# The last adaLN gate of a decoder block: its partial rows summed into a column layout instead of a broadcast row

## What is computed

```python
mod = jax.nn.silu(c) @ w_ada[l] + b_ada[l]
sh_m, sc_m, gt_m, sh_f, sc_f, gt_f = [m[:, None, :] for m in jnp.split(mod, 6, axis=-1)]
...
x = x + gt_m * rms_norm(mix, g_post_mix[l])
h = rms_norm(x, g_pre_ffn[l]) * (1.0 + sc_f) + sh_f
ff = peer_ffn(h, peer_wq[l], peer_k1[l], peer_k2[l], peer_u[l], peer_v[l])
x = x + gt_f * rms_norm(ff, g_post_ffn[l])
```

## Time and profile before

| what | value |
|---|---|
| median of three runs | 1837.81 us (1836.92 to 1838.18) |
| the profiled execution, its own time | 1838.79 us |
| span from its first to its last instruction | 1836.8 us |
| TensorE busy with matmuls | 1788.0 us, 97% of the span |
| VectorE busy | 1586.4 us, 86% |
| ScalarE busy | 825.0 us, 45% |
| GpSimd busy | 207.1 us, 11% |
| DMA | 617.98 MB, mean 336 GB/s |
| mean granted TensorE clock | 0.994 of full speed |

### The profile page before, as it was taken

How to read it: one execution, slowest core, us unless ns; L and a number is a source line. 1 busy time by engine, 2 the same in 40 slices (tenths; PEclk the granted TensorE clock), 3 DMA queues, 4 the chain that set the end, 5 groups by cost and what they waited for, 6 DMA issues and landing times.

```text
span 1836.8 us, 28930 instructions
## 1 busy us (share of the span) xinstructions
PE 1788.0 (97%) x9874; PEld 1565.2 (85%) x9874; DVE 1586.4 (86%) x2605; ACT 825.0 (45%) x1187; POOL 207.1 (11%) x193
## 2 busy tenths in 40 slices
PE   6999999998999999999999999989999999999998
PEld 6878888444999999999999999988888888888886
DVE  4669899966678999999999999987888888888887
ACT  3011222302635555333566666554555455555544
POOL 1000000110000000111121111121111111111110
PEclk9999999999999999999999999999999999999999
DMA  9998766798686677998999999999999999999995
GB/s 385 421 422 340 273 252 251 290 421 365 229 324 252 230 250 252 365 338 325 339 352 363 359 362 363 347 364 342 382 368 371 364 375 366 363 368 376 363 373 211
DMA packets 96785, 617.98 MB, mean 336 GB/s; under 512 B 11697, under 2 KB 20433, under 8 KB 25041
## 3 DMA queue, kind: packets, MB, share of 16 engines
q1 hardware_dynamic: 60048, 415.26, 59.0%
q0 software_dynamic: 25408, 184.58, 26.3%
q10 hardware_dynamic: 11266, 17.32, 2.5%
HBM read 600.26 MB, written 16.79 MB: 336 GB/s over the span
## 4 chain that ended last, share of the span: by engine, by line
PE 71%; DVE 13%; DMA 11%; issue 4%; ACT 1%; DVEq 0%; SPq 0%; ACTq 0%
PE ps L1310 32%; PE ps L960 12%; PE ps L967 8%; DMA raw<-in_w_ada 7%; PE ps L1005 6%; PE ps L1168 4%; PE ps L1114 3%; DVE big L1390 2%; PE ps L1016 2%; PE ps L1262 2%; DVE raw L1415 2%; DVE w_low L1368 2%; DMA big<-in_u_rows,row_ix 2%; DMA big<-in_w_gate_f 1%; DVE big L1471 1%
## 5 line engine op out<-in xcount | busy, mean ns | idle before, releaser
L673 ACT ACTIVATE w_hi<-raw 128x1024 fp32r<-128x1024 f32 x520 | 551.4, 1061 | 499.9 <-PE ps L1310 245.3
L1368 DVE TENSOR_TENSOR w_low<-raw,w_hi 128x1024 fp32r<-128x1024 f32 x520 | 631.8, 1220 | 96.5 <-ACT w_hi L673 89.6
L1310 PE MATMUL ps<-w_hi,a 128*128 128x512 f32 x1536 | 391.3, 390 | 5.6 <-DVE a L1823 5.6
L960 PE MATMUL ps<-a,w_hi 128*128 128x384 f32 x1856 | 374.1, 342 | 0.9 <-issue 0.8
L1310 PEld LDWEIGHTS ps<-w_hi,a 128*128 128x128 f32 x1536 | 289.1, 188 | 66.2 <-issue 5.8
L960 PEld LDWEIGHTS ps<-a,w_hi 128*128 128x128 f32 x1856 | 315.9, 189 | 1.9 <-issue 1.7
L1310 PE MATMUL ps<-w_low,a 128*128 128x512 f32 x1024 | 274.8, 390 | 0.0
L967 PEld LDWEIGHTS ps<-a,w_low 128*128 128x128 f32 x1856 | 237.7, 191 | 10.1 <-DVE w_low L1368 9.5
L967 PE MATMUL ps<-a,w_low 128*128 128x192 f32 x1856 | 241.8, 272 | 4.0 <-DVE w_low L1368 3.6
L1310 PEld LDWEIGHTS ps<-w_low,a 128*128 128x128 f32 x1024 | 192.6, 188 | 40.7 <-DVE w_low L1368 0.7
L1415 DVE CUSTOM_DVE_ANT_0 raw<-raw,big 128x2048 f32<-128x2048 f32 x64 | 146.2, 2290 | 66.7 <-DMA raw<-in_w_ada 64.0
(11 more groups left out here) (224 smaller groups left out, 1665.4 us busy)
## 6 DMA issues: line engine op xcount, KB each, us to landing
raw<-in_peer_u SPq DMA_DIRECT2D x128, 1024.0 KB
raw<-in_peer_v SPq DMA_DIRECT2D x128, 1024.0 KB
early<-in_w_front SPq DMA_DIRECT2D x56, 1024.0 KB, 9.0
raw<-in_w_ada POOLq DMA_DIRECT2D x48, 1024.0 KB, 9.1
raw<-in_w_ada SPq DMA_DIRECT2D x32, 1024.0 KB, 12.6
raw<-in_peer_wq SPq DMA_DIRECT2D x16, 1024.0 KB
big<-in_w_gate_f SPq DMA_DIRECT2D x16, 1024.0 KB, 7.2
gel_saved<-stage ACTq DMA_DIRECT2D x64, 192.0 KB
```

Source lines behind the costliest of these rows:

```text
L673: act.activation(w_hi[:, h % 2, :], raw[:, s % RING, :], ACT.Copy).then_inc(hi_ready, 1)
L960: done = pe.matmul(ps[:, b % 2, 0:2 * TD].rearrange("p (m t) -> p m t", m=2), w_hi[:, ph.nth(j) % 2, k * P:(k + 1) * P], a_pair[:, kc, :, ...
L1310: done = pe.matmul(ps[:, 4 * tt + 2 * (j % 2) + n, :], a, w[:, n * 512:(n + 1) * 512], start=i is None and blk == 0 and m in (0, 2), stop= ...
L1368: dve.tensor_tensor(w_low[:, s % RING, :], raw[:, s % RING, :], w_hi[:, h % 2, :].bitcast(F32), ALU.subtract).then_inc(lo_ready, 1)
```

## The change

The partial rows are summed the other way round: the partial rows are the stationary operand and a single column of ones is the moving one. Sixteen products take the place of four. Product kc loads the 128 columns of `acc_last` that lie 16 numbers apart, starting at kc, and gives 128 sums on 128 partitions, one per partition, in column kc of bank 4. The gate then lies as 128 partitions x 16 numbers, and partition q holds the numbers 16q to 16q + 15.

The norm weights come in the same layout as an input of their own, `g_gate_cols`, 8 KB instead of the 1024 KB broadcast, and their load is issued on ScalarE's queue without the wait for `gate_made`. VectorE does one product of 128 x 16 instead of four of 128 x 512. The store to `gate_saved` becomes 128 runs of 64 bytes instead of one row; the bytes in DRAM and the load back stay as they were.

```diff
+        gate_col, g_gate = sb("gate_col", [P, KC]), sb("g_gate", [P, KC])
...
             put_y(PAIRS - 1)
-            act.wait_ge(gate_made, 4)
-            act.dma_start(g_row, rows[3, :].partition_broadcast(P)).then_inc(g_row_in, 16)
+            act.dma_start(g_gate[:, :], g_gate_cols).then_inc(g_gate_in, 16)
...
                 if j == 11:
-                    act.wait_ge(gate_f_made, 4)
-                    act.dma_start(gate_saved, gate_row[0:1, :]).then_inc(gate_f_saved, 16)
+                    act.wait_ge(gate_f_made, 1)
+                    act.dma_start(gate_saved.rearrange("o (q k) -> q (o k)", k=KC), gate_col[:, :])\
+                        .then_inc(gate_f_saved, 16)
...
                     pe.wait_ge(ada_used, 2 * KC)
-                    for g in range(4):
-                        done = pe.matmul(ps[:, 4 + g, :], ones[:, :], acc_last[:, g * 512:(g + 1) * 512], start=True,
+                    for kc in range(KC):
+                        done = pe.matmul(ps[:, 4, kc:kc + 1], acc_last.rearrange("p (q k) -> p k q", k=KC)[:, kc, :], ones[:, 0:1], start=True,
                                          stop=True)
                     done.then_inc(gate_f_sum, 1)
...
                     for g in range(4):
-                        pe.wait_ge(gate_f_made, g + 1)
+                        pe.wait_ge(gate_f_made, 1)
...
                 dve.wait_ge(gate_f_sum, 1)
-                dve.wait_ge(g_row_in, 32)
-                for g in range(4):
-                    cols = slice(g * 512, (g + 1) * 512)
-                    dve.tensor_tensor(gate_row[:, cols], ps[:, 4 + g, :], g_row[:, cols], ALU.mult)\
-                        .then_inc(gate_f_made, 1)
+                dve.wait_ge(g_gate_in, 16)
+                dve.tensor_tensor(gate_col[:, :], ps[:, 4, 0:KC], g_gate[:, :], ALU.mult).then_inc(gate_f_made, 1)
...
+        "g_gate_cols": np.ascontiguousarray(np.asarray(g_post_ffn)[0].reshape(P, KC)),
+        "rows": np.stack([b[2], b[5], np.asarray(g_post_mix)[0]]),
```

More of the change, by code:

```diff
@@ L117, with build_block @@
 AXX = mybir.AxisListType.X
-def build_block(nc, x, c, c_row, w_ada, w_gate_f, b_cols, g_cols, rows, w_front, lambdas, g_subln, conv_w,
+def build_block(nc, x, c, c_row, w_ada, w_gate_f, b_cols, g_cols, g_gate_cols, rows, w_front, lambdas, g_subln, conv_w,
                 conv_vecs, peer_wq, peer_keys, peer_u, u_rows, peer_v, out):
@@ L267, in build_block @@
                                                        sem("last_bias_in"))
+        g_gate_in = sem("g_gate_in")
         late_in, g_row_in = sem("late_in"), sem("g_row_in")
@@ L1962 @@
         "g_cols": np.ascontiguousarray(np.stack([columns(g) for g in (g_pre_mix, g_pre_ffn)], axis=1)),
-        "rows": np.stack([b[2], b[5], np.asarray(g_post_mix)[0], np.asarray(g_post_ffn)[0]]),
+        "g_gate_cols": np.ascontiguousarray(np.asarray(g_post_ffn)[0].reshape(P, KC)),
+        "rows": np.stack([b[2], b[5], np.asarray(g_post_mix)[0]]),
         "w_front": np.concatenate([w[:, n_qkv:].reshape(KC, P, D), np.stack(qkv), mix]),
```

## The result

The changed kernel is slower, by 0.25%: 1843.42 us, median of 7 runs (1839.51 to 1844.85), against 1838.18 us for the kernel before in the same series. The ratio is 1.0025, 95% interval 1.0015 to 1.0035. The forecast was 1837.7 us, no change, with a range up to 1841.5.

What follows compares the result with a forecast made beforehand. TensorE was taken as the main bound (71% of the span), with transfers of `w_ada` late from 359 to 391 us. +0.11 - 0.39 + 0.14 = -0.14 us on 1838.79 us, or 1837.7 us on the median; range 1835.5 to 1841.5.

Steps and rivals of the forecast that it cites:

- Step 1: TensorE's sum at unit 6: 32 one-column passes at 0.112 us, 3.57 us, replace 3.46 us, so +0.11 us.
- my own sign: Profile check on the sum's line: about 3.6 us expected; under 2 or over 6 us fells the pass estimate.
- The upper end: Upper bound for the sum's passes: each load exposed at 0.190 us, 6.08 us for 32, +2.6 us.
- Step 2: Sum's stationary loads pick numbers 64 bytes apart: no cost taken, +1.3 us kept for the range.
- rival (a): Sum's passes cost moderately more, load exposed or stride up to about twice: +0.1 to +3.8 us net; 25%.
- rival (b): Stride makes each load wait for every line: slower beyond 0.2%, at four times +10.6 us, 1848.4 us; 9%.
- Rival (c): TensorE's clock falls while the sum's passes stream next to nothing: about 2.6 us, 1840.3 us; 5%.
- the case of both at once: Moderately dearer passes and a fallen TensorE clock together, counted as slower; 1%.
- Step 3: VectorE's four products become one: about 2.2 us of its time goes, ending a TensorE stall worth 0.39 us.
- Steps 4 and 5: Dropped 1 MB load worth 0, bound -0.5 us; small load issued earlier among late transfers costs +0.14 us.
- Step 6: Store to `gate_saved` in 128 runs, and changed waits, cost nothing; GpSimd's gathers at 729.1 us wait for indices anyway.

Runs made afterwards that it cites:

- dense: Changed kernel with each stationary operand read from 128 neighbouring numbers instead of 128 numbers 64 bytes apart; passes 3.69 us, ratio to the kernel before 1.0009.
- wide: Changed kernel with 128 moving columns of ones instead of one, strided loads kept; passes 7.01 us, ratio to the kernel before 1.0018.
- oldsum: Changed kernel with the four old TensorE products put back and all else kept; passes 3.46 us, ratio to the kernel before 1.0000.
- step2: Changed kernel with the 128 numbers of each stationary operand 8 bytes apart; run once for its profile, about 0.12 us per pass at full clock.

## Why the prediction was wrong

**Step 1, the passes.** The term was right for what it priced: 0.112 us per dense pass, and dense loads took 3.60 us with 128 columns and 3.69 us with one. By my own sign, passes of over 6 us, this step would fall; `dense` shows that it is the next one. The upper end, an exposed load of 0.190 us, is refuted by `dense`.

**Step 2, the stride. This step failed.** It was taken at nothing, with +1.3 us as its bound, on the factor of 1.33 from a strided read of VectorE. The measured factor is about two, 0.214 against 0.112 us, and the term is +3.4 us. I had named the Trainium skill's rule on lines, which speaks against the edit, and gave the operand that breaks it no cost because no row showed one. That two engines read strides alike was the assumption, and it had no support. The stride at this price was in rival (a), with 25%, and alone it would have stayed within the range; rival (b), four times, overstated it, and its threshold of 0.23 us per pass lies just over the measured 0.214.

**Rival (c), the clock, was true** and stood at 5%. Its price of 2.6 us was somewhat high (1.6 and 2.1 measured). Two reasons against it failed. "Loads are work too": in `wide` and in the changed kernel the loads are the same and the streamed columns differ, and the clock fell only in the kernel with one. "It was still full after 3 us nearly empty": so it was there, but in `dense`, where the passes lasted about the 3.6 us that I had in mind, the clock fell as well.

**The rivals were taken as nearly exclusive.** Each of them alone ends under 1841.5 us: the stride with 1841.1 (1837.7 + 3.4), the clock with 1840.3. Together, and less the stall, they are the +4.55 us of the stretch, 1842.4 us against the median of 1837.81, outside the range. Both come from the same line, so the case of both at once needed a chance of its own and a sum; it had a share of 1%.

**Step 3** was right: the product takes 0.168 us, the stall is gone, -0.40 us in `oldsum` against -0.39 forecast. **Steps 4 and 5**: the small load's +0.14 us is not to be seen, and neither is a gain from the load that went. The second mixing half started 0.10 us earlier, but this says little of 0.14 us: in `dense`, which is the same up to there, VectorE's products of line 1589 began at 387.4 us, 1.2 us earlier than in the profile of the changed kernel (388.6), and TensorE did not wait for them. **Step 6** was right: GpSimd's first gather started at 732.6 us and waited for the indices, not for the store.

## What to carry to other kernels

A sum over the partitions costs by passes: swapping a few wide products for many one-column products brings as many weight loads, and gains nothing even when the loads are dense (3.60 to 3.69 against 3.46 us). If the operands are swapped, lay the data out so that the stationary operand reads neighbours, and let more than one column move with it (128 did here), or the products that follow may pay for the clock (1.4 to 2.1 us here). VectorE work that was saved (2.3 us here) is worth only the wait that it ended, 0.4 us.

## What the runs showed of the hardware that I had not expected

The pace of the strided loads did not go with the clock. In the changed kernel the passes come every 0.214 us before and after the clock falls at about 583.5 us (9 of them in 580 to 582 us, 32 in 6.7 us), whereas in `step2` the passes stretch once the clock is low (min/median/max ns, between 583 and 584 us, against 256 ns above):

```profile
L1230 PE MATMUL ps<-ones,big x6: 352/352/353, 582.7 to 583.8; 128*128 128x1 f32 x6
```

There they come every 0.22 us, the pace of the strided loads at full clock. TensorE's profile calls itself busy throughout (3.00 of 3.00 us in the fences above) while the clock is taken away, so the busy share gives no warning of it.

And a reduction over partitions on GpSimd held one operation of VectorE for nearly its whole length, 215.56 of 226.4 us, though the two work on different data.
